# Two-block transformer kernel: the weights' low parts are subtracted on the vector engine instead of GpSimd, with one norm between the blocks and the parameter loads on SyncE's queue

## The reference, cut to what matters

```python
def reference(x, ...):
    x = first_block(x, meta_tokens, ..., final_g)    # 2 layers: 24 attention heads, gates, branches; then rmsnorm with final_g
    return second_block(x, mix_norm_g_2, ...)        # 2 layers of token mixers; layer 0 a dense FFN, layer 1 a mixture of experts

for l in range(DEPTH):                               # second block
    h = rmsnorm_2(x, mix_norm_g[l])
    x = x + token_mixers(h, ...)                     # retention, SSD, GLA, mLSTM; 32 gate tiles; w_branch, w_out
    h = rmsnorm_2(x, ffn_norm_g[l])
    x = x + (swiglu(h, ...) if l % 2 == 0 else moe_ffn(h, ...))
return rmsnorm_2(x, final_norm_g)
```

## Time and profile before

| what | value |
|---|---|
| median of three runs | 2702.86 us |
| the profiled execution | 2700.96 us, its span 2699.1 us |
| PE busy | 2446.2 us, 91% |
| DVE busy | 1521.1 us, 56% |
| ACT busy | 1269.0 us, 47% |
| POOL busy | 877.4 us, 33% |
| mean granted clock of PE | 0.951 |

### The profile page before, as it was taken

One profiled execution on the slowest core, in us unless ns is written; L12 is line 12 of the kernel. 1 busy time (PEld: TensorE's weight loads), 2 busy tenths in 40 slices (PEclk: granted clock), 3 DMA queues, 4 the chain that ended last, 5 costly groups with the idle time before them and its releaser, 6 DMA issues.

```text
span 2699.1 us, 38592 instructions
## 1 busy us (share of the span) xinstructions
PE 2446.2 (91%) x15110; PEld 2048.7 (76%) x15110; DVE 1521.1 (56%) x2267; ACT 1269.0 (47%) x1802; POOL 877.4 (33%) x394
## 2 busy tenths in 40 slices
PE   7999989999968979778998879868999999999998
PEld 6877778877767868668997868767777777777775
DVE  2244462244553543672012553684998898899896
ACT  4524434534524342423222342423777677677664
POOL 4643355644445554444553554341000000000000
PEclk8999999999988989979998989978999999999999
DMA  5432233433253433333443333323999899899993
GB/s 159 142 111 79 95 110 118 143 112 95 94 121 110 119 118 94 99 113 128 161 164 117 112 125 94 96 93 154 375 355 346 331 355 347 332 351 352 332 350 147
DMA packets 255355, 489.14 MB, mean 181 GB/s; under 512 B 35096, under 2 KB 208696, under 8 KB 221128
## 3 DMA queue, kind: packets, MB, share of 16 engines
q1 hardware_dynamic: 227440, 483.74, 51.1%
q10 hardware_dynamic: 27080, 1.22, 0.7%
q0 software_dynamic: 656, 1.71, 0.2%
HBM read 485.57 MB, written 1.05 MB: 180 GB/s over the span
## 4 chain that ended last, share of the span: by engine, by line
PE 65%; DVE 13%; ACT 3%; issue 2%; DMA 1%; POOL 1%; ACTq 1%; DVEq 0%; SPq 0%
PE bank L1018 21%; PE bank L683 18%; PE bank L708 9%; PE bank L551 4%; PE bank L533 2%; DVE mem_high L2038 2%; PE bank L971 2%; DVE mem_high L2237 1%; PE bank L590 1%; DVE memr L1830 1%; PE bank L489 1%; PE bank L722 1%; PE bank L1059 1%; PE bank L658 1%; DVE mem_high L2194 1%
## 5 line engine op out<-in xcount | busy, mean ns | idle before, releaser
L1018 PE MATMUL bank<-memr 128*128 128x256 f32 (+5 forms) x8016 | 1075.3, 295 | 133.0 <-DVE mem_high L1974 27.2
L1018 PEld LDWEIGHTS bank<-memr 128*128 128x128 f32 (+3 forms) x8016 | 1018.1, 193 | 181.8 <-issue 44.1
L1384 POOL TENSOR_TENSOR memr<-mem_low,memr 128x1024 fp32r<-128x1024 f32 (+2 forms) x316 | 755.1, 2390 | 845.1 <-ACT memr L1461 833.3
L877 DVE TENSOR_TENSOR memr_tail<-mem_tail,memr_ring 128x2048 fp32r<-128x2048 f32 x198 | 452.1, 2290 | 60.6 <-ACT memr_ring L774 57.4
L683 PE MATMUL bank<-memr_ring,memr 128*104 128x512 f32 x1492 | 467.8, 399 | 3.1 <-DVE memr L882 3.1
L774 ACT CAST memr_ring<-mem_tail 128x2048 fp32r<-128x2048 f32 x198 | 379.4, 1917 | 130.8 <-PE bank L683 89.1
L1461 ACT CAST memr<-mem_low 128x1024 fp32r<-128x1024 f32 (+2 forms) x316 | 324.4, 1041 | 236.8 <-PE bank L1018 214.5
L683 PEld LDWEIGHTS bank<-memr_ring,memr 128*104 128x104 f32 x1492 | 250.8, 168 | 95.4 <-issue 3.3
L708 PE MATMUL bank<-memr_ring,memr 128*104 128x512 f32 x752 | 242.3, 400 | 1.7 <-DVE memr_ring L877 1.7
L683 PE MATMUL bank<-memr_tail,memr 128*104 128x512 f32 x536 | 211.6, 395 | 0.0
L708 PEld LDWEIGHTS bank<-memr_ring,memr 128*104 128x104 f32 x752 | 125.3, 168 | 42.9 <-DVE memr_ring L877 1.9
(11 more groups left out here) (241 smaller groups left out, 2598.7 us busy)
## 6 DMA issues: line engine op xcount, KB each, us to landing
mem_tail<-in_moe SPq DMA_DIRECT2D x198, 1024.0 KB, 4.9
mem_low<-in_w_in SPq DMA_DIRECT2D x112, 1024.0 KB, 5.1
mem_high<-in_moe SPq DMA_DIRECT2D x33, 1024.0 KB, 4.8
mem_low<-in_moe SPq DMA_DIRECT2D x33, 1024.0 KB, 4.9
mem_high<-in_ffn_w SPq DMA_DIRECT2D x30, 1024.0 KB, 8.2
mem_low<-in_w_branch SPq DMA_DIRECT2D x20, 1024.0 KB, 5.0
mem_low<-in_w_out SPq DMA_DIRECT2D x16, 1024.0 KB, 5.3
mem_low<-in_w_in SPq DMA_DIRECT2D x6, 512.0 KB, 3.9
```

The costliest lines, as they stand in the source:

```text
L877: TTn(raw_r[n % RAW], raw[n % RAW], hi_f[n % HI], ALU.subtract).then_inc(family("m_split"), 1)
L1018: ins = pe.matmul(out(bank), lhsT, rhs, start=((k, i) == order[0]), stop=((k, i) == order[-1]))
L1384: pl(pool.tensor_tensor(low, raw, high, ALU.subtract), sig("w_split", i))
```

## The change

1. POOL's `low_parts` and its MLP loop are gone. DVE gets `low_until(n)`, which subtracts tiles up to number n, each behind its `w_high`. It is called at chosen places of DVE's list: `ready(name)` does the tiles up to the one that the product `name` needs and then waits for the product; `low_after(name)` does the tiles that ACT had cast before it began the casts that follow the product `name` (`cast_before`); `low_gates(n)` does this for the next n gate products. In the MLP, `low_up(F)` stands behind the hidden tile two steps earlier.
2. The two norms between the blocks become one. With f the first block's gain and g the second's, y = x f r1 and y r2 g is x (f g) / sqrt(mean(x^2 (f^2 + eps)) + eps^2). PE sums the squares with a weight matrix f^2 + eps in place of ones. The plain sum of squares still comes, right behind it; DVE scales x2 by it later, tile by tile, in the heads' loop of the second block's layer 0.
3. The 27 parameter loads go to SP's queue, up to six behind each of five chunks, from the fifth chunk of the branch weights of the first block's last layer.
4. In the MLP's start ACT takes the norm's root before the first casts, not behind them.

```diff
             for l in range(DEPTH):                      # POOL
-                low_parts(before_gates[l])
-
                 pool.wait_ge(*at("c_ready", l))
...
-            for F in range(NF):
-                pool.wait_ge(*at("up_high", F))
-                for m in range(2):
-                    _, raw, high, _, low = up_parts(F, m)
-                    pl.settle()
-                    pl(pool.tensor_tensor(low, raw, high, ALU.subtract), sig("up_split", F) if m else None)
...
             def follow(*name):                          # ACT
                 full(act, *name)
+                cast_before[name] = high_no[0]
                 if tile_use[tile_of[name]][1:] == name:
                     ahead(*name)
...
-                        for dst, src in later[(n * KT + j) * 2:(n * KT + j + 1) * 2]:
-                            act.dma_start(dst, src, allow_slow_non_contiguous=True).then_inc(*sig("params2", by=16))
...
+            def low_until(until):                       # DVE
+                while low_no[0] < until:
+                    i = low_no[0]
+                    low_no[0] += 1
+                    s_, c0, c1 = tiles[i]
+                    n, kt, c, _ = splits[s_]
+                    dve.wait_ge(*at("w_high", i))
...
+                    st(V.tensor_tensor(low, raw, high, ALU.subtract), sig("w_split", i))
+            def low_after(*name):
+                low_until(cast_before.get(name, 0))
+            def ready(*name):
+                low_until(tile_of.get(name, -1) + 1)
+                return full(dve, *name)
...
             def silu_tile(l, j):
-                b = full(dve, "z", l, j)
+                b = ready("z", l, j)
...
+                low_after("z", l, j)
...
+            low_until(AHEAD - 1)
             for l in range(DEPTH):
                 normalise(("ss", l), 0, f"norm_g{l}", ...)
-                b = full(dve, "ff", l)
+                for nm in ("fq", "fk"):
+                    for j in range(4):
+                        low_after(nm, l, j)
+                for c in range(2):
+                    low_after("fv", l, 2, c)
+                b = ready("ff", l)
...
                     if i >= 2 and i % 2 == 0:
                         gated(g // 2 - 1)
+                    low_after("g", l, i)
...
                 st(TTn(rowb[32:36, :], rowb[32:36, :], tsc[32:36, 2, 0:T], ALU.add), sig("rows_ready", l))
+                low_gates(GATES_BEFORE[0])
                 for j in range(10):
                     conv_silu(l, j)
...
                     pick(n)
+                    low_gates(GATES_LEVEL[n])
...
+                low_gates(3)
                 st.settle()
                 for n in range(4):
                     for j in range(KT):
-                        b = full(dve, "br2", l, n, j)
+                        b = ready("br2", l, n, j)
...
             mid = chunks_before_ffn[0]                  # SP
+            later = param_dmas[n1:]
             for n in range(mid):
+                if n == params2_from[0]:
+                    sp.wait_ge(*at("o_full", 12 * DEPTH - 1))
+                    sp.wait_ge(*at("y_ready", 12 * DEPTH - 1))
                 ring_chunk(n)
+                if n >= params2_from[0]:
+                    for dst, src in later[:6]:
+                        sp.dma_start(dst, src, allow_slow_non_contiguous=True)...
+                        later = later[1:]
...
-                norm2(("mix", l))                       # PE
+                if l:
+                    norm2(("mix", l))
+                else:
+                    pe.wait_ge(*at("final_w"))
+                    sum_squares(("ss2", ("mix", l)), ("mix", l), T, lambda k: pc("final_w", k).broadcast_to((P, P)))
+                    sum_squares(("ss", DEPTH), ("mix", l), T)
```

More of the change, by code:

```diff
@@ L1052, in rope2, with sum_squares @@
                 gemm(("rot", *name), [(const("rot64"), asc[:, rope_no[name] % 2, 0:T])], lambda b: b[:, 0:T])
-            def sum_squares(name, key, n, lo=0):
+            def sum_squares(name, key, n, weights=None):
                 bank = open_group(name)
@@ L1169, in _ @@
                 after_gates[l] = len(tiles)
+                params2_from[0] = len(chunks) + NSLOT
                 for n in range(3):
@@ L1494, in squares, with root @@
                     if k == 0:
-                        st(A(stat[0:1, 1, 14:15], eps[0:1, :], ACT.Sqrt))
+                        st(A(stat[0:1, 1, 14:15], eps[0:1, 0:1], ACT.Sqrt))
                     st(A(sq[:, k, lo:n], src[:, k, lo:n], ACT.Square), sig("squares", key, k))
-            def root(name, slot, dim, n=TA, lo=0):
+            def root(name, slot, dim, n=TA, least=0, lo=0):
                 b = full(act, *name)
-                st(A(rstd[:, slot, lo:n], b[:, lo:n], ACT.Sqrt, bias=eps[:, 0:1], scale=1.0 / dim), free(*name))
+                st(A(rstd[:, slot, lo:n], b[:, lo:n], ACT.Sqrt, bias=eps[:, least:least + 1], scale=1.0 / dim), free(*name))
             for l in range(DEPTH):
@@ L1643, in norm2 @@
                     then()
-                root(("ss2", key), 0, D, T)
+                root(("ss2", key), 0, D, T, least)
             def rope_raw2(name):
@@ L1864, in _ @@
                 st(V.tensor_scalar(tsc[0:8, 3, :], tsc[0:8, 1, :], -(64 ** 0.5), None, ALU.mult), sig("c_ready", l))
-                for j in range(6):
+                for j in range(4):
                     silu_tile(l, j)
+                for j in range(5):
+                    low_after("cq", l, j)
+                silu_tile(l, 4)
+                silu_tile(l, 5)
                 def rope(name, m, cos, sin, mat_src, outs, done, c0=m0):
-                    b = full(dve, *name)
+                    b = ready(*name)
                     st.settle()
@@ L1968, in _ @@
                     for j in range(KT):
-                        b = full(dve, "br", l, n, j)
+                        b = ready("br", l, n, j)
                         if n == 0 and j == 0:
@@ L2017, in rope2 @@
             def rope2(name, dst):
-                b = full(dve, "rot", *name)
+                b = ready("rot", *name)
                 st.settle()
@@ L2025, in gate2 @@
             def gate2(l, j):
-                b = full(dve, "gz", l, j)
+                b = ready("gz", l, j)
                 dve.wait_ge(*at("gz_tanh", l, j))
@@ L2133, in _ @@
                 for t in range(2):
-                    b = full(dve, "sxt", l, t)
+                    b = ready("sxt", l, t)
                     st(S3(out=vtok[:, 1, t, :].rearrange("p (h c) -> p h c", h=4),
@@ L2244, in _ @@
                 for j in range(KT):
-                    b = full(dve, "wo2", l, j)
+                    b = ready("wo2", l, j)
                     st(S3(out=x2[:, j, :], in0=b[:, 0:T], scalar=0.5, in1=x2[:, j, :], op0=ALU.mult, op1=ALU.add),
                        free("wo2", l, j))
+                    low_after("wo2", l, j)
                 if l == 0:
@@ L2253, in _ @@
                 if l == 0:
+                    for F in range(NHIGH):
+                        low_up(F)
                     for F in range(NF):
```

154 lines of the change are left out of this document (98 added, 56 removed).

## The result

The changed kernel takes 2598.35 us (median of four runs, 2595.95 to 2598.96), the kernel before, in runs beside it, 2702.02 us (2693.6 to 2704.74). The profiled execution took 2598.0 us with a span of 2596.2.

A forecast was written before the change was run, and what follows sets the result against it. PE, busy 91% of the span, bounds the kernel, and its waits on DVE hide POOL's subtractions; the terms sum to -71 us, from 2701 to 2630 (2631 on the median's scale), range 2600 to 2680.

The forecast's parts named there:

- (i): The rest: MLP with its start and seam -1 us, short waits on POOL -5, PE's clock -10 (0 to -20).
- (a): ACT's parameter loads: PE's 14.4 us wait shrinks to 1.8 and layer 1's clock rises; -18 us (-13 to -24).
- (b): Between the blocks: one norm for two, 16.9 us becomes 7.0; with PE's clock -11 us (-8 to -14).
- (c): GLA levels: DVE still sets the period, 4.9 us becoming 4.43; -7 us (0 to -16).
- (e): Convolutions: PE's waits of 8.1 and 7.2 us shrink, the tile of gz 5 comes 2.3 late; -8 us (+4 to -14).
- (f): Row scans: gate product 2 waits for the chain, the next tiles subtracted only after it; +4 us (-6 to +15).
- (g): Logarithm chain: z product 1's tile is subtracted only after DVE's first SiLU; +4.2 us a layer, +8 (0 to +15).
- (h): First block's branch sums: DVE's work becomes 29 us beside PE's 26, collisions go; -8 us (0 to -15).
- first rival: Parameter loads stall SP as they stall ACT, costing 8 us and a lower clock behind them: 2640 to 2645; chance 0.08.
- collisions weren't POOL's: Rival: POOL doesn't cause the collisions, so levels, sums and convolutions turn to their costs: 2731 us; chance 0.02.
- DVE-bound heads: Rival: in the softmax heads DVE's delay exceeds 2.06 us and each head pays a subtraction: 2719 us; chance 0.05.
- More won: Rival: levels, sums and clock come out at their far bounds: 2600 us; chance 0.10.

The follow-up runs named there:

- e2: The changed kernel with the 27 parameter loads issued by ACT again, two behind each product of the branches: 2610.69 us, ratio 0.9673.
- e5: The changed kernel with the weight tiles of gate products 2 and 3 subtracted behind the row-scan chain, not before it: 2609.35 us, ratio 0.9667.
- e1: The changed kernel with the subtraction of the low parts given back to POOL, the rest of the change kept: 2681.99 us, ratio 0.9939.
- e7: The changed kernel with subtractions moved at four places where PE waits for them, among them the MLP's first tile beside the norm's sum: 2576.92 us, ratio 0.9542.
- e3: The changed kernel plus four unneeded POOL subtractions of 128x256 behind each cast of a second-block mixer weight tile: 2704.11 us, ratio 1.0018.
- e4: The changed kernel with one more DVE operation of the same shape ahead of each of the 316 mixer-tile subtractions: 2789.71 us, ratio 1.0334.
- e6: The changed kernel plus four unneeded POOL memsets of 128x256, without reads, behind each cast of a second-block mixer weight tile: 2600.48 us, ratio 0.9636.
- e8: The changed kernel plus two unneeded POOL subtractions of 128x256 behind each cast of a second-block mixer weight tile: 2640.84 us, ratio 0.9784.

## Why the prediction was off, step by step

The direction and the mechanism were right: POOL sat on the chain under DVE's name. The size was short by 33 us. By stages, the two spans differ by 102.9 us; the prediction's clock and short waits (i) are inside the measured column, since each stage has them in it.

| step | forecast | measured by stage |
|---|---|---|
| (a) loads | -18 | -13 (e2) |
| (b) one norm | -11 | -9.9 |
| (c) GLA levels | -7 | -8.5 |
| (d) heads' scaling, branch sums | -15 | -16 |
| output product of the second block | not in the list | -11.4 |
| (e), (f) convolutions and row scans | -4 | -26 |
| (g) logarithm chain, first block's projections | +8 | -1 |
| (h) first block's branch sums | -8 | -15 |
| (i) MLP | -1 | -0.7 |
| clock and short waits | -15 | in the rows above |

The measured column adds up to -101.5; the remaining 1.4 us are the start and the heads.

**The step that failed is (f), with (e).** "DVE's list has the tiles up to gate product 2, then waits for ACT, then runs the whole chain, and only then subtracts the next." That is not the list. ACT casts the tiles of gate products 2 and 3 behind the first half of `gv`, and so `low_after("gv", l, 1)` subtracts them ahead of the chain. e5 puts them where the prediction had them: 11.7 us of the 22 that the step missed. The rest is what the prediction had at hand and didn't carry through. It wrote that the scans go from 6.11 to 2.0 us, and they did (1.98), but it charged four subtractions against it and left PE's wait at its old size; it fell from 8.8 to 0.88 us in the rows of e5 above (2.4 of it came back in the wait behind it, 2.7 us for 0.3). In (e) it left 1.5 of 4.0 us at the first place and found nothing left there. The waits of 2.28 us for `gz` 5 came as forecast, twice.

**The size of the collisions.** 150 to 200 us were assumed from the two-input groups, 235 to 252 were there. The prediction's condition, "both inputs in SBUF", was too narrow: in e1 even L1999, an operation with one input of three columns, is held for 0.57 us on average, and the first step of a convolution sum, one input too, takes 1073 ns and not 411. This is where (h), the output product, whose first products wait for held-up low parts of the sums, and the rotary products in (g) came out better. Which of these operations gave how much of each stage is argued and not shown; that it was collision and not late low parts is shown by PE's waits for POOL, 6.1 us in all. The gain of (g) hides a wait that was forecast rightly: PE stands 4.9 and 5.1 us for the subtraction behind the logarithm chain, for which +8 was taken, and the projections still got no longer, because the collisions in them went at the same time.

**(i), the MLP's start.** -2 was forecast, and it got some 1.4 us longer. The subtraction, which POOL did beside the norm, now stands behind the norm's sixteen operations of DVE: 11.0 us of wait in one piece, 14.0 us behind the last tile of the output product. In the kernel before PE waited 5.2 us there, did one product and waited 3.9 more, so that its work began in earnest 12.6 us behind that tile. Only from the first product on does the start look 5.8 us longer and the rest 6.5 shorter. e7 took the wait back with a cast and a subtraction ahead of the norm.

**(a)** was 5 us too dear: the clock of layer 1 was taken up to that of layer 0, 0.98, and it came to 0.95 in both layers. **(b)** and **(c)** are right: 800.84 to 807.86 us between the blocks (7.0, as forecast), and a level's period of 4.24 us for 4.43. The level's rows, with PE's wait of 0.47 where the earlier trace rows has 1.16:

```profile
1047.93 1.22 DVE L1837 TENSOR_TENSOR memr<-mem_low,memr 128x1024 fp32r<-128x1024 f32 x1
1048.03 1.04 ACT L1452 CAST memr<-mem_low 128x1024 fp32r<-128x1024 f32 x1
1048.19 0.73 PE L513 MATMUL bank<-mem_high 32*128 32x128 f32 x16 [0.47 <-DVE mem_high L2270]
```

**The rivals.** The first rival had the mechanism and not the price. The loads do hold SP up (issues of 3.9, 5.5 and 6.4 us), and one chunk landed after 9.5 us in place of some 5, but the reserve, put at 10 us, covered it, and PE got all that the loads had cost (e2). The Trainium skill's rule ("DMA: Bandwidth & Descriptors", section "Queues, rings and completion order") is that each DMA engine takes the descriptors of a ring in their order; with it the prediction put up to 5.6 us ahead of a chunk, for which it shows no working. The trace agrees with the rule: that chunk came 4 us late. That the collisions weren't POOL's fell with e1 and e3. The DVE-bound heads didn't come, but the price of nothing rested on the wrong slack: "2.06 us are free" was measured from p to PE's use of it, while what the subtraction delays is the next head's maximum. A subtraction fits there almost to the last 0.2 us; e4 shows 0.87 us a head for the next 1.22. The rival had 0.05, and its cliff was 1.2 us away, not beyond 2.7.

"More won", 2600 at the far bounds of levels, sums and clock, is what came, with 0.10 on it; its bounds were too near as they rested on the same sizes as the forecast.

## What to carry to other kernels

Where one form of operation has two durations, far apart, in one trace, add up what the slow ones lose over the whole span before costing the change: here some 240 of DVE's 1521 us were such time, and the engine that caused it had 1% of the chain. Read from the code at which event each moved step can run, tile by tile, before calling its wait late. And take the slack of a moved step from what stands next in its own engine's list, not from the consumer of what stood there before it.

## What the runs showed of the hardware

- A POOL operation with two SBUF inputs holds up DVE's operations whose operands all lie in SBUF, down to 128x3, until POOL's is over: the level's first product takes 2183 ns beside operations of 2.4 us, 425 without them. Forms with an operand in a PSUM bank aren't held: 422 ns in both kernels (L2312, L2341). POOL's writes without a read (e6, 312 ns each) leave the convolution step at 486 ns. The Trainium skill, "SBUF — State Buffer", section "Who interferes with whom", says the same of two-input operations against reads, and names copies and scalar operations in the two-port modes as the one-input case; L1970 and L1999 may be such, 169 and 738 ns.
- One row doesn't fit that page, by which an operation with at most one SBUF input, outside those modes, isn't held. The first step of a convolution sum has one SBUF input and takes 411 ns in the changed kernel, as long as an operation with two inputs of that size (the 128x256 scalar operation of the row chain takes 0.29 us), and still 1073 ns in e1 (767 in e3, 617 in e8, 428 in e6). Its two factors come from SBUF too; whether that is the reason was not tried.
- An issue of a load of many single numbers can hold its queue for microseconds: 6.31 us on ACT in the kernel before, up to 6.38 us on SP in the changed one. The same loads cost 12 to 13 us where casts stand behind them (e2) and nothing that PE sees where weight chunks do.
- PE takes 48 products of the reduced 32-bit format with 256 columns in 5.95 us, 124 ns each, and 32 of plain float32 in 7.07 us, 221 ns each (changed kernel, at 1025.10 and 800.84 us).
